# Projections of a two-stage transformer block: three split products or one plain float32 product

## What is computed

```python
for l in range(2):                                    # first block
    mod = silu(c) @ w_mod[l] + b_mod[l]               # 2048 -> 6144: shift, scale, gate
    h = rmsnorm(x) * (1 + scale) + shift
    proj = h @ w_in[l]                                # 2048 -> 7504 columns
    y = sparse_attention(...), retention(...)         # from proj
    x = x + gate * (y @ w_out[l])                     # 2048 -> 2048
h = rms_norm(x); proj = h @ w_in_2                    # second block, 2048 -> 7176
x = x + (stick_breaking(...), forgetting(...)) @ w_out_2
q = rms_norm(x) @ peer_w_query_2                      # picks 16 of 16384 experts per head and row
x = x + sum over 8 heads, 16 picks of gate * gelu(u[pick] . h) * v[pick]
```

## Time and profile before

| what | value |
|---|---|
| median of 3 runs | 3126.39 us (3125.57 to 3129.42) |
| span of the profiled execution | 3121.8 us, 29077 instructions |
| around the span (median less span) | 4.6 us |
| TensorE busy, mean granted clock | 2089.0 us (67%), 0.830 |
| VectorE / ScalarE / GpSimd busy | 1836.5 / 853.8 / 800.9 us |
| moved by DMA | 900.90 MB, mean 289 GB/s |

### The profile page before, as it was taken

How to read it: one execution, slowest core, us unless ns; L and a number is a source line. 1 busy time by engine, 2 the same in 40 slices (tenths; PEclk the granted TensorE clock), 3 DMA queues, 4 the chain that set the end, 5 groups by cost and what they waited for, 6 DMA issues and landing times.

```text
span 3121.8 us, 29077 instructions
## 1 busy us (share of the span) xinstructions
PE 2089.0 (67%) x11378; PEld 1478.6 (47%) x11378; DVE 1836.5 (59%) x2711; ACT 853.8 (27%) x1267; POOL 800.9 (26%) x680
## 2 busy tenths in 40 slices
PE   5888989989999999999999983223232322322235
PEld 2676777888787787666668871000000000000001
DVE  3679886566776664343336697766565555564430
ACT  1334544444454454544545420000000000000000
POOL 1111110000000000000000036665555555555552
PEclk8999999999999999999999996566656566666667
DMA  9887875557665545334226699999999999999998
GB/s 385 289 293 263 296 259 150 184 182 248 210 189 153 164 158 172 111 122 132 85 82 201 194 377 403 422 422 421 421 422 421 422 421 419 421 421 421 421 421 346
DMA packets 244741, 900.90 MB, mean 289 GB/s; under 512 B 20759, under 2 KB 45613, under 8 KB 178413
## 3 DMA queue, kind: packets, MB, share of 16 engines
q0 software_dynamic: 94208, 612.85, 48.9%
q1 hardware_dynamic: 149152, 284.53, 27.8%
q10 hardware_dynamic: 1244, 1.67, 0.2%
HBM read 894.78 MB, written 2.10 MB: 287 GB/s over the span
## 4 chain that ended last, share of the span: by engine, by line
PE 45%; DMA 29%; DVE 10%; ACT 3%; issue 3%; POOL 2%; ACTq 0%; POOLq 0%; DVEq 0%
PE pp L1818 38%; DMA late<-in_peer_v,MI 9%; DMA P<-in_peer_v,MI 5%; PE tp L1818 5%; DMA x<-in_peer_v,MI 5%; DMA ring<-in_peer_v,MI 4%; DVE wL L1130 3%; DMA SY<-in_peer_v,MI 2%; PE tp L1821 2%; ACT wH L626 1%; DMA ring<-in_peer_w_query 1%; DVE UHM L1286 1%; DMA ring<-in_w_in 1%; POOL late L2361 1%; DVE P L1777 0%
## 5 line engine op out<-in xcount | busy, mean ns | idle before, releaser
L1130 DVE TENSOR_TENSOR wL<-ring,wH 128x1024 fp32r<-128x1024 f32 (+3 forms) x504 | 583.2, 1161 | 573.7 <-ACT wH L626 572.4
L1818 PE MATMUL pp<-wH,hH 128*128 128x512 f32 (+3 forms) x1888 | 745.7, 395 | 35.5 <-DVE wL L1130 19.4
L1818 PE MATMUL pp<-wL,hH 128*128 128x512 f32 (+3 forms) x1888 | 721.4, 382 | 0.0
L1818 PE MATMUL pp<-wH,hL 128*128 128x512 f32 (+3 forms) x1888 | 720.5, 382 | 0.0
L626 ACT ACTIVATE wH<-ring 128x1024 fp32r<-128x1024 f32 (+3 forms) x504 | 508.3, 1011 | 729.7 <-PE pp L1818 548.0
L1818 PE MATMUL pp<-late,S 128*32 128x512 f32 x768 | 232.6, 879 | 335.7 <-DMA x<-in_peer_v,MI 156.3
L1818 PEld LDWEIGHTS pp<-wH,hH 128*128 128x128 f32 x1888 | 362.3, 192 | 141.2 <-issue 46.3
L1818 PEld LDWEIGHTS pp<-wH,hL 128*128 128x128 f32 x1888 | 361.6, 192 | 64.1
L1818 PEld LDWEIGHTS pp<-wL,hH 128*128 128x128 f32 x1888 | 362.8, 192 | 57.3 <-issue 1.0
L1777 DVE CUSTOM_DVE_ANT_0 late<-late,P 128x2048 f32<-128x2048 f32 x84 | 191.2, 2288 | 155.2 <-DMA late<-in_peer_u,MI 155.2
L1818 PE MATMUL pp<-P,S 128*32 128x512 f32 x360 | 162.7, 898 | 166.9 <-DMA late<-in_peer_v,MI 93.2
(11 more groups left out here) (305 smaller groups left out, 2985.2 us busy)
## 6 DMA issues: line engine op xcount, KB each, us to landing
ring<-in_w_in SPq DMA_DIRECT2D x288, 512.0 KB, 4.4
ring<-in_w_out SPq DMA_DIRECT2D x96, 512.0 KB, 4.2
P<-in_w_mod POOLq DMA_DIRECT2D x85, 512.0 KB, 5.1
late<-in_w_mod SPq DMA_DIRECT2D x64, 512.0 KB, 9.4
SY<-in_w_mod POOLq DMA_DIRECT2D x43, 512.0 KB, 5.5
ring<-in_w_in SPq DMA_DIRECT2D x48, 368.0 KB, 4.8
ring<-in_peer_w_query SPq DMA_DIRECT2D x32, 512.0 KB, 7.9
ring<-in_w_in SPq DMA_DIRECT2D x24, 344.0 KB, 3.2
```

Source lines behind the costliest of these rows:

```text
L1130: tt(lo, raw, hi.bitcast(F32), ALU.subtract).then_inc(*tick("dve_lo", *names))
L1818: return e.matmul(o, l, r, start=start, stop=stop, skip_group_check=skip)
```

## The change

The splits go. The activations are kept once, in `hT` (float32), and a piece multiplies them with the raw weights where they were loaded, one float32 matmul call where there were three of float32r. A piece's ring slot is now free when its matmuls are done. The ring grows from 4 to 11 slots, and the loads run 8 pieces ahead (3 before). Three more buffers of the same tile hold w_mod's later blocks (`NM`); its first 64 use eight of the ring's slots. The lane rate of w_mod in layer 0 goes from 1.12 to 0.7. Of a chunk of four turned blocks ScalarE writes the first two to `hT` and VectorE the other two, at the same time, and a piece waits only for its own half. The experts have 14 slots; slots 5 and 6 are in `hT` and wait for the last group.

```diff
-NB, NS, NG = 3, 4, 11
+NS, NM, NG = 11, 3, 14
+AHEAD = NS - 3
...
-    def splits(p, q):
-        while asked[0] < min(place[p, q] + NB, len(where)):
-            yield "split", *where[asked[0]]
+    def fetches(p, q):
+        while asked[0] < min(place[p, q] + AHEAD, len(where)):
+            yield "fetch", *where[asked[0]]
...
         yield from project(2 * l, after_in, lambda n: (0.7 if n < 14 else 1.0, 0.6 if n < 12 else 0.85,
-                                                       1.12 if l == 0 else 0.45), early_out)
+                                                       0.7 if l == 0 else 0.45), early_out)
...
-        ring = sb("ring", [128, NS, 1024])
+        ring = sb("ring", [128, NS + NM, 1024])
...
-        with ExitStack() as early:
-            hH = early.enter_context(nc.sbuf_tensor("hH", [128, NK, 256], FR))
-            hL = early.enter_context(nc.sbuf_tensor("hL", [128, NK, 256], FR))
-            wH = [early.enter_context(nc.sbuf_tensor(f"wH{j}", [128, 1024], FR)) for j in range(NB)]
-            wL = [early.enter_context(nc.sbuf_tensor(f"wL{j}", [128, 1024], FR)) for j in range(NB)]
-        late = sb("late", [128, 8192])
+        hT = sb("hT", [128, NK, 256])
...
-        mod_in = [*[late[:, 1024 * b:1024 * b + 1024] for b in range(8)], P[:, 0, GA:GA + 1024], P[:, 1, GA:GA + 1024],
-                  SY[:, 1536:2560]]
+        mod_in = [*[ring[:, NS - 8 + b, :] for b in range(8)], *[ring[:, NS + b, :] for b in range(NM)]]
...
         gs = [P[:, 0, 4400:6448], P[:, 1, 4096:6144], SY[:, 0:2048], x[:, 0, :], x[:, 1, :],
-              rf[:, 0:2048], rf[:, 2048:4096], *[late[:, 2048 * b:2048 * b + 2048] for b in range(4)]]
+              hf[:, 0:2048], hf[:, 2048:4096], *[rf[:, 2048 * b:2048 * b + 2048] for b in range((NS + NM) // 2)]]
...
                 if r >= NS:
                     w.wait_ge(*at("ring used", r - NS))
+                elif r >= NS - 8:
+                    w.wait_ge(*at("mod used", 56 + r - (NS - 8)))
...
-            def split(p, q):
-                n, c0, wd, pc = PIECES[p][q]
-                r, k = next(loads), next(cut)
-                raw = heads(ring[:, r % NS, 0:2 * wd], 2)
-                w.wait_ge(*at("raw", r))
-                if k >= NB:
-                    w.wait_ge(*at("cut used", k - NB))
-                act(heads(wH[k % NB][:, 0:2 * wd], 2), raw, ACT.Copy).then_inc(*tick("act_hi", ("hi", k)))
...
-                            else:
-                                for m in (189, 190, 191) if p else (157, 158, 159):
-                                    w.wait_ge(*at("mod used", m))
...
+                        if n:
+                            w.wait_ge(*at("squared", p, n - 1, t))
...
+                        if (t, g) != (0, 0):
+                            w.wait_ge(*at("attended", l, *((t, 0) if g else (t - 1, 1))))
...
-                tt(lo, raw, hi.bitcast(F32), ALU.subtract).then_inc(*tick("dve_lo", *names))
...
+                    for j in (2, 3):
+                        k = 4 * c + j
+                        ts(hT[:, k, :], tp[u % 2][:, j * 256:j * 256 + 256], mcol[:, l, 16 + k:17 + k], mcol[:, l, k:k + 1],
+                           ALU.mult, ALU.add).then_inc(*tick("dve_h", *([("chunk turned", u), ("chunk", p, c, 1)] if j == 3 else [])))
...
-            def three(o, l, r, first, final, skip=False):
-                mm(o, l[0], r[0], first, False, skip)
-                mm(o, l[0], r[1], False, False, skip)
-                return mm(o, l[1], r[0], False, final, skip)
...
-                w.wait_ge(*at("lo", k))
-                w.wait_ge(*at("chunk", p, pc // 2))
+                w.wait_ge(*at("raw", r))
+                w.wait_ge(*at("chunk", p, pc // 2, pc % 2))
...
-                        hs = hH[:, kk, t * 128:(t + 1) * 128], hL[:, kk, t * 128:(t + 1) * 128]
-                        m = three(pp[b][:, 0:wd], hs, (hi[:, k2, :], lo[:, k2, :]), kk == 0, kk == 15)
-                    names = [("cut used", k)] if t else []
+                        m = mm(pp[b][:, 0:wd], hT[:, kk, t * 128:(t + 1) * 128], raw[:, k2, :], kk == 0, kk == 15)
+                    names = []
+                    if t and not (p == 4 and meta_part(c0, wd)):
+                        names.append(("ring used", r))
...
-                            ws = hi[:, k2, b * 128:(b + 1) * 128], lo[:, k2, b * 128:(b + 1) * 128]
-                            m = three(pr6[:, b * 256:(b + 1) * 256], ws, (hH[:, kk, :], hL[:, kk, :]),
-                                      kk == 0 and b % 2 == 0, kk == 15, True)
-                    m.then_inc(*tick("pe_piece", ("cut used", k), *([("grouped", 6, n)] if pc == 7 else [])))
+                            m = mm(pr6[:, b * 256:(b + 1) * 256], raw[:, k2, b * 128:(b + 1) * 128], hT[:, kk, :],
+                                   kk == 0 and b % 2 == 0, kk == 15, True)
+                    m.then_inc(*tick("pe_piece", ("ring used", r), *([("grouped", 6, n)] if pc == 7 else [])))
...
                 elif slot == 5:
-                    w.wait_ge(*at("lo", LAST_CUT))
-                elif slot == 7:
                     w.wait_ge(*at("grouped", 6, 3))
...
-                if m in (64, 160):
-                    w.wait_ge(*at("chunk", 2 * l if m == 160 else 0, 3))
```

More of the change, by code:

```diff
@@ L195, in project @@
         for q, (n, c0, w, pc) in enumerate(PIECES[p]):
-            yield from splits(p, q)
+            yield from fetches(p, q)
             if p in (0, 2) and n == 0:
@@ L324, in order @@
     for q, (g, c0, w, pc) in enumerate(PIECES[6]):
-        yield from splits(6, q)
+        yield from fetches(6, q)
         if q == 3:
@@ L512, in slots, with parts @@
                 had[i] = n
-        def parts(p, c):
-            step = 2 if p in (1, 3) and c < 2 else 1
-            return [(k, step) for k in range(4 * c, 4 * c + 4, step)]
+        def parts(p, k0):
+            step = 2 if p in (1, 3) and k0 < 8 else 1
+            return [(k, step) for k in range(k0, k0 + 2, step)]
         def gain(p, k):
@@ L536, in mixer_peer_program @@
         SLOTS = list(slots())
-        LAST_CUT = sum(len(p) for p in PIECES) - 1
         def mod_slot(m):
@@ L582, in sync @@
             for what, *a in order():
-                if what == "split":
+                if what == "fetch":
                     p, q = a
@@ L616, in store_rows @@
                                     xP[q:128:4, t, d * 512:(d + 1) * 512]).then_inc(*landed(sem, ("out", t, d, q)))
[L617 to L626 removed]
+            turn, side = itertools.count(), itertools.count()
             def norm(p):
@@ L1101, in vector @@
             tt, stt, copy, recip = e.tensor_tensor, e.scalar_tensor_tensor, e.tensor_copy, e.reciprocal
-            turn, loads, cut = itertools.count(), itertools.count(), itertools.count()
+            turn = itertools.count()
             def ts(o, a, s1, s2, op0, op1):
@@ L1764, in vector @@
                     for b0 in (0, 8):
-                        next(loads)
                         u = next(turn)
@@ L1813, in tensor @@
         def tensor(e, w):
-            turn, side, loads, cut = itertools.count(), itertools.count(), itertools.count(), itertools.count()
-            had_pair, had_bank = {}, {}
+            turn, side, loads = itertools.count(), itertools.count(), itertools.count()
+            had_pair, had_bank, by_two = {}, {}, set()
             def mm(o, l, r, start, stop, skip=False):
@@ L1855, in piece @@
                 n, c0, wd, pc = PIECES[p][q]
-                k = next(cut)
-                hi, lo = (heads(b[k % NB][:, 0:2 * wd], 2) for b in (wH, wL))
-                w.wait_ge(*at("lo", k))
-                w.wait_ge(*at("chunk", p, pc // 2))
+                r = raw_of[p, q]
+                raw = heads(ring[:, r % NS, 0:2 * wd], 2)
+                w.wait_ge(*at("raw", r))
+                w.wait_ge(*at("chunk", p, pc // 2, pc % 2))
                 for t in range(2):
@@ L1865, in piece @@
                         kk = pc * 2 + k2
-                        hs = hH[:, kk, t * 128:(t + 1) * 128], hL[:, kk, t * 128:(t + 1) * 128]
-                        m = three(pp[b][:, 0:wd], hs, (hi[:, k2, :], lo[:, k2, :]), kk == 0, kk == 15)
-                    names = [("cut used", k)] if t else []
+                        m = mm(pp[b][:, 0:wd], hT[:, kk, t * 128:(t + 1) * 128], raw[:, k2, :], kk == 0, kk == 15)
+                    names = []
+                    if t and not (p == 4 and meta_part(c0, wd)):
+                        names.append(("ring used", r))
+                    elif t and pc % 2:
+                        names += [("ring used", raw_of[p, q - 1]), ("ring used", r)]
                     if pc == 7:
@@ L2253, in tensor @@
             gathers = itertools.count()
-            raw_of, cut_of, side_use, ahead = {}, {}, [0], [itertools.count()]
+            raw_of, side_use = {}, [0]
             lanes = Lanes(dict(tables=tables, mods=mods, meta_sum=meta_sum, sparse=sparse, gate=gate, gate_rows=gate_rows,
@@ L2263, in tensor @@
```

(17 more changed lines are left out.)

63 lines of the change are left out of this document (19 added, 44 removed).

## The result

The changed kernel takes 3272.25 us (median of 4 runs, 3270.68 to 3273.46) against 3126.06 (median of 4): a ratio of 1.047, 95% interval 1.0451 to 1.0489. It is slower by 146 us, where +209 was forecast and 3300 us was the lower end. Sign and main term hold; the size is off by 63 us.

A forecast was written before the change was run, and what follows sets the result against it. TensorE was taken to bound projections 0 to 5 and DMA the gathers. Product +314, waits -78, clock -18, chunks -3 and gathers -6 us sum to +209 on 3126.4, giving 3335 us, range 3300 to 3385.

The forecast's parts named there:

- The product: Projections 0 to 5: plain float32 products, two records of 0.43 us at 512 columns, cost TensorE +314 us.
- The rival that priced a pass at 0.227: Projections: each of four float32 passes costs a float32r matmul's 0.227 us, term 403, total 3424 us; chance 0.04.
- not slower: Whole kernel: products cheaper than the trace's, records 0.37 us apart or less; 3021 us at 0.34; chance 0.02.
- The lane waits stay: Projections: VectorE and ScalarE chains keep their lengths, only wL and a little clock come back; 3410 us; chance 0.12.
- Waits: Projections 0 to 5: of TensorE's 106 us idle time, -78 us comes back, bounds -19 to -106.
- three quarters of the other 87 us less the norm boundaries: Projections: share of TensorE's idle time beyond the wL waits expected to go, about 59 us.
- the spread of w_mod at no gain: Layer 0: w_mod at 0.7 steps per piece was given no cost and no term in the sum.
- The rest of the stage: Projections 0 to 5: slow clock -18 us, bounds 0 and -27, and chunks -3 us, bounds 0 to -10.
- if half of the 106 idle us lie in these 99: Projections: premise about time at the lower clock, giving some 50 us of slow work that loses 25.
- Projection 6 and gathers: After the six projections: no change up to the first gather, then -6 us in the gathers' stretch.
- Even: Projection 6 up to the first gather: dearer matmuls and the splits' removal balance, no change in time.
- five query loads leave the stretch: Gathers' stretch: query loads still to come fall from 17 to 12, worth -6 us at 420 GB/s.

The follow-up runs named there:

- e2: Kernel before with splits, buffers and order kept, but each product one plain float32 matmul of the two high parts: 3349.18 us, ratio 1.0705.
- e8: e1 with w_mod's lane in layer 0 back at 1.12 steps per piece: 2985.24 us, ratio 0.9548 to the kernel before.
- e5: Changed kernel with w_mod's lane in layer 0 at the old 1.12 steps per piece: 3283.57 us, ratio 1.0509 to the kernel before.
- e1: Changed kernel with three float32r matmuls per product from one fixed buffer, no split, weights left out of products, 10 ring slots: 2963.26 us, ratio 0.9487.
- e4: Changed kernel with loads 3 pieces ahead in the written order, not 8: 3272.5 us, ratio 1.0463 to the kernel before.
- e6: Changed kernel with 7 ring slots for the weights in place of 11: 3285.8 us, ratio 1.052 to the kernel before.
- e3: Kernel before, but VectorE makes the weights' remainder for only 16 columns from the 41st piece on: 3058.98 us, ratio 0.9772.

## Why the prediction was wrong in size

**The product, right.** +314 forecast, +310.9 measured; 0.43 us a record forecast, 0.429 measured. The constant operand of the ones product and the turned output of the index scores were good stand-ins for a stream from `ring`. The Trainium skill's count of four passes for true float32 ("FP8 and Floating Point Precision", section TensorE Precision Notes) fits the two records of a call with 0.215 us a pass at 512 columns. The rival that priced a pass at 0.227 is out. So is "not slower": the records would have had to be 0.37 apart. "The lane waits stay" (3410) is out too.

**Waits, mis-sized.** -78 forecast, -95.9 measured. The step that failed is "three quarters of the other 87 us less the norm boundaries": nearly all went. Part of that was a wrong reading: the four waits on P L1192 lie at 504, 557, 1012 and 1065 us, at stores of w_in's gate groups, and not at a change of projection, and they went. The reason I gave first, the longer pieces, was the weaker one: alone it takes 55 us (e2), while e8 takes 83 with short pieces and w_mod at its old rate. And I had set the spread of w_mod at no gain; it is 11 us by e5, 8 of them idle time in a single wait.

**The rest of the stage, the largest miss.** -21 forecast (clock -18, chunks -3), -56 measured. The step that failed is "if half of the 106 idle us lie in these 99", from which followed 50 us of slow work and a loss of 25. The trace's own record of the granted clock has it at half for 108 us of the stage, as the mean of 0.967 asks, and only 20 of these are idle. So 88 us of work ran slow and lost 44. In the changed kernel 14 us are at the lower clock, 3 of them idle, which loses 5. That is -39 where the forecast had -18, outside its bound of -27. The longest wait of the kernel before shows why so few of the slow microseconds are idle (columns as in the earlier trace rows):

```profile
184.00:188.00 4.00, 0.15 (x2) 0.00 (x0) 3.32 (x3) 1.60 (x3) 0.53 (x1) 1.00 1.00 354
188.00:193.00 5.00, 0.00 (x0) 0.00 (x0) 4.84 (x9) 1.06 (x1) 1.06 (x2) 0.51 1.03 396
193.00:198.00 5.00, 4.95 (x14) 4.08 (x15) 1.89 (x2) 0.00 (x0) 0.53 (x1) 0.50 0.88 306
```

TensorE stands idle for the first 4 us at the full clock, then for 5 us at the lower one, and the 5 us of work behind the wait run slow.

The other 17 us had -3 for the chunks. About 11 are steps just before or behind a wait at the full clock, each priced against the median of its like: they take 13 us too long before, 2 in e1 and 1 in the changed kernel. I had no term for them. And at most 7 belong to the form of the products, the difference in the rest between e1 (287.0) and the changed kernel (280.4). What the chunks gave isn't shown.

It would be easy to take too much for the form. Behind a transpose, a float32r record has a longer distance to the next one than in its stream. The kernel before, then the changed kernel:

```profile
214.19 1.05 PE L1818 MATMUL tp<-MI,TAB 128*128 128x128 f32 x8
214.99 0.48 PE L1818 MATMUL pp<-wH,hH 128*128 128x512 f32 x1
215.31 0.40 PE L1818 MATMUL pp<-wL,hH 128*128 128x512 f32 x1
```
```profile
204.38 1.05 PE L1771 MATMUL tp<-MI,TAB 128*128 128x128 f32 x8
205.28 3.60 PE L1771 MATMUL pp<-ring,hT 128*128 128x512 f32 x8
```

From 214.99 to 215.31 are 0.32 us, where the stream has 0.227; a plain record in the same place takes 0.432 against 0.429. But the float32r record also starts earlier: 0.80 us behind the start of the eight transposes, where the plain one starts after 0.90. From the start of the last transpose of 128 columns to the second product record the median is 0.344 us with float32r (68 places before, 80 in e1) and 0.541 with plain float32 (80 places). The streams make 0.110 + 0.227 = 0.337 and 0.110 + 0.429 = 0.539. So such a switch costs 2 to 7 ns in either form. Over all 159 switches to a product of 512 columns in e1 and in the changed kernel, the mean over both sides differs by 5 ns more than the streams do, under 1 us in the stage.

**Projection 6 and gathers.** "Even" was +3.7 us, as the pieces run full length now with TensorE never waiting. The gathers gave -14.4 where I had -6. The step that failed is "five query loads leave the stretch", from 17 to 12: I counted by the pieces ahead in the written order, and the slots count (e4). Between the first gather and the 23rd, SyncE issued 16 query loads before, with 4 slots, and 9 after, with 11. The stretch before, to be held against 1960:2027 of the changed kernel above:

```profile
1797.00:1877.00 80.00, 63.78 (x459) 60.69 (x458) 71.27 (x97) 20.84 (x21) 29.10 (x22) 0.91 0.98 380
```

DMA was nearly full in both. The query loads moved 8.4 MB there before and 5.1 after; 3.3 MB are 8 us at 420 GB/s, of the 12 by which the stretch is shorter. The other 4 go with the rate, 380 GB/s before and 403 after. The wait of the 23rd gather for its slot was 2.45 us before and is 2.20 after, so it isn't what the change gained; e6 shows what it costs where it is long. The first gather and the 23rd:

```profile
1959.68 1.01 POOL L2310 DMA_INDIRECT P<-in_peer_u,MI  x1 [40.11 <-DVE MI L1594]
...
2027.00 2.76 POOL L2310 DMA_INDIRECT hT<-in_peer_u,MI  x1 [2.20 <-PE tp L1771]
```

These are 67 us, where the earlier trace rows have 80; I had worked out 69 to 70 for it from pieces and bytes, and did not see that 80 before against 70 after was already a gain of ten.

In the sum: product -3, waits -18, slow clock -21, other matmuls and restarts -14, way to the gathers +4, gathers -8, and 2 us by which the runs lie closer together than the spans: within rounding the 63 us.

**Open.** The chunks by halves were not tried by themselves, nor was w_mod in buffers of its own. Which part of e1's gain is the splits' and which the slots' and chunks' is known only as far as e3, e6 and e8 tell. Why the lower clock holds for as long as it does behind a wait was not tried.

## What to carry to other kernels

Where one engine sets a stage, price a change of its instructions by starts in a stream, and add beside it everything else in that engine's time: idle, slow clock, and the steps next to a wait; together they gave back 152 us here, half of what the dearer product cost. Take the slow clock from the work that lies in it and not from the idle time. Read a switch between two kinds of matmul over both of its sides, since the record behind it can start early and seem long. A wait can have more than one sufficient cause: at one rate of w_mod, two remedies that take 83 and 55 us alone took 88 together. How far a queue runs ahead is set by its buffers and not by where the loads stand in the written order.

## What the runs showed of the hardware

- A float32 product of 512 columns in two records of 0.429 us against three float32r of 0.227 each: 26% more, at 256 columns 0.432 against 0.360, 20% more. A float32r matmul has some 13 ns on top of its columns at the full clock and none at the lower one (0.307 us for 368 columns is 368 at 1.2 GHz); a plain record has 2 ns at the full clock.
- Behind a transpose of 128 columns a float32r record of 512 starts 0.03 us after the transpose's start and is 0.31 us ahead of the next; a plain one starts after 0.11 and is 0.43 ahead. In the sum neither is more than 7 ns above the streams.
- The lower clock fell mostly on work: of 108 us at it in the kernel before 20 were idle, and the work in the others lost 44 us.
- Late small loads behind gathers cost by the wait they hold up: in e6, 2 MB more in the stretch took 18 us, of which the bytes are 5 at 420 GB/s.
